# Hybrid attention and convolution encoder on one core: the first norm in fewer steps, identity products moved, the fifth weights' rounding amid the logarithms, and VectorE's order around unit 3

## The reference

```python
def encoder_layer(x, ...):
    h = rmsnorm(x, norm_mix)
    proj = einsum('btd,de->bte', h, w_in)
    q, k, v, r, g_lr, hy_in = split(proj, ...)
    o_gla = gla_group(q, k, v, r, g_lr, ...)     # gates: log_sigmoid(z @ w + b) / 16, cumulative sums
    o_hy = hyena_group(hy_in, ...)               # filters: hid = sin(freq * (feats @ w1 + b1)), twice
    x = x + einsum('bte,ed->btd', concatenate([o_gla, o_hy]), w_out)
    h = rmsnorm(x, norm_ffn)
    return x + (silu(h @ w_gate) * (h @ w_up)) @ w_down
```

## Time and profile before

| | us |
|---|---|
| median of 3 runs | 1246.21 (1244.27 to 1246.93) |
| the profiled execution, its own time | 1245.52 |
| its span (first to last instruction) | 1243.7 |
| TensorE busy | 1227.4 |
| GpSimd, ScalarE, VectorE busy | 756.9, 729.1, 726.2 |

### The profile page before, as it was taken

One profiled execution on the slowest core, in us unless ns is written; L12 is line 12 of the kernel. 1 busy time (PEld: TensorE's weight loads), 2 busy tenths in 40 slices (PEclk: granted clock), 3 DMA queues, 4 the chain that ended last, 5 costly groups with the idle time before them and its releaser, 6 DMA issues.

```text
span 1243.7 us, 21588 instructions
## 1 busy us (share of the span) xinstructions
PE 1227.4 (99%) x8224; PEld 1022.6 (82%) x8224; DVE 726.2 (58%) x1072; ACT 729.1 (59%) x1345; POOL 756.9 (61%) x618
## 2 busy tenths in 40 slices
PE   8999999999999999999999999999999999999997
PEld 6767787889988888888887777788898888888886
DVE  6846576677777777300068465664867777760004
ACT  6766655448577767532266756554576777763333
POOL 3755653547488667866527666328265666778661
PEclk9999999999999999999999999999999999999999
DMA  6211111251323322332222212114122222324232
GB/s 240 81 52 53 69 52 69 69 191 52 102 103 103 102 102 85 118 104 97 97 77 69 69 52 70 67 54 141 63 86 102 103 102 103 116 77 139 92 102 85
DMA packets 31496, 115.31 MB, mean 93 GB/s; under 512 B 3489, under 2 KB 4001, under 8 KB 31010
## 3 DMA queue, kind: packets, MB, share of 16 engines
q1 hardware_dynamic: 31394, 113.93, 26.6%
HBM read 111.82 MB, written 2.10 MB: 92 GB/s over the span
## 4 chain that ended last, share of the span: by engine, by line
PE 86%; DVE 8%; ACT 4%; issue 2%; POOL 0%; DMA 0%; POOLq 0%; ACTq 0%; DVEq 0%
PE ps L2166 19%; PE ps L2173 11%; PE ps L2006 6%; PE ps L2025 6%; PE ps L2028 6%; PE ps L2026 6%; PE ps L2008 6%; PE ps L2007 6%; PE ps L2332 2%; PE ps L2318 2%; PE ps L2019 2%; PE ps L2017 2%; PE ps L2022 2%; PE ps L2192 1%; PE ps L2169 1%
## 5 line engine op out<-in xcount | busy, mean ns | idle before, releaser
L1257 POOL TENSOR_TENSOR w_lo<-w_raw,w_hi 128x1024 fp32r<-128x1024 f32 x104 | 254.7, 2450 | 260.3 <-ACT w_hi L716 203.5
L716 ACT ACTIVATE w_hi<-w_raw 128x1024 fp32r<-128x1024 f32 x108 | 114.0, 1056 | 173.8 <-PE ps L2028 157.8
L2166 PE MATMUL ps<-h_parts,w_hi 128*128 128x512 f32 x576 | 204.9, 398 | 0.0
L2173 PE MATMUL ps<-h_parts,w_lo 128*128 128x256 f32 x672 | 188.8, 281 | 0.0
L2006 PE MATMUL ps<-h_parts,w_hi 128*128 128x512 f32 (+1 forms) x392 | 166.2, 424 | 1.9 <-POOL w_lo L1257 1.0
L2166 PE MATMUL ps<-sum_parts,w_hi 128*128 128x512 f32 x432 | 156.3, 402 | 0.0
L2008 PE MATMUL ps<-h_parts,w_lo 128*128 128x512 f32 (+1 forms) x392 | 151.9, 388 | 0.0
L2007 PE MATMUL ps<-h_parts,w_hi 128*128 128x512 f32 (+1 forms) x392 | 151.3, 386 | 0.0
L2173 PE MATMUL ps<-sum_parts,w_lo 128*128 128x256 f32 x528 | 148.4, 281 | 0.0
L1262 POOL TENSOR_TENSOR w_lo<-w_raw,w_hi 128x512 fp32r<-128x512 f32 x60 | 77.7, 1296 | 97.6 <-ACT w_hi L702 97.6
L702 ACT ACTIVATE w_hi<-ps 128x512 fp32r<-128x512 f32 x160 | 94.6, 597 | 61.0 <-DVE ps L1518 39.0
(11 more groups left out here) (300 smaller groups left out, 2844.1 us busy)
## 6 DMA issues: line engine op xcount, KB each, us to landing
w_raw<-in_units SPq DMA_DIRECT2D x110, 512.0 KB, 3.2
u<-in_pairs SPq DMA_DIRECT2D x44, 512.0 KB, 3.9
w_raw<-in_pairs SPq DMA_DIRECT2D x40, 512.0 KB, 4.1
x<-in_x SPq DMA_DIRECT2D x4, 512.0 KB, 6.4
gain<-in_gain SPq DMA_DIRECT2D x4, 512.0 KB
spec<-in_pairs SPq DMA_DIRECT2D x4, 512.0 KB, 5.1
out_y<-x SPq DMA_DIRECT2D x3, 512.0 KB, 2.6
par<-in_par SPq DMA_DIRECT2D x1, 1214.5 KB, 8.0
```

The costliest lines, as they stand in the source:

```text
L716: nc.scalar.activation(w_tile(g, 0), w_raw[:, g % RAW], ACT.Copy).then_inc(s_hi, 1)
L1257: nc.gpsimd.tensor_tensor(w_tile(g, 1), w_raw[:, g % RAW], w_tile(g, 0).bitcast(F32), ALU.subtract).then_inc(s_lo, 1)
L2166: nc.tensor.matmul(both(m, p).rearrange("p (v t) -> p v t", v=2), hi[:, cols], factor[m][:, :, k], start=start and k == 0, stop=False, ski ...
L2173: last = nc.tensor.matmul(both(m, p)[:, FIRST] if p >= WIDE else out, lo[:, cols], factor[m][:, 0, k], start=False, stop=k == KT // 2 - 1, ...
```

## The change

Six things are different.

- The first norm: `first_square` squares a whole tile of 1024 columns in one instruction, `first_root` takes the root of sum/1024 + eps with eps from a column that GpSimd sets; VectorE's mean step is gone.
- ScalarE's order at the start: w_hi of unit 0 ahead of the roundings of tiles 0 and 1, w_hi of unit 1 behind the rounding of tile 3.
- TensorE: identity products 2, 4, 4 in place of 8, 2, 8 around the first transposes; the turns of tiles 2 and 3 both behind the first half of unit 0, then five identity products into bank 1, the second half, and only then the first product of the filter network.
- The 1 MB of constants (`K_DFT` on) is issued behind the load of unit 2's weights and so behind that load's wait.
- w_hi of unit 4 is made between the Exp and the Ln of `gate_logs` in layer 0.
- VectorE, slot 2: first the unit with index 2 (the third; q) is emptied, then comes the first scan pair, then the second range reduction (layer 0), then the second scan pair.

```diff
+                if L == 0 and n == RAW:
+                    sp.dma_start(cst[:, K_DFT:N_CST], cst_d[:, K_DFT:N_CST]).then_inc(s_dft, 16)
...
+            def first_square(tt):
+                act.wait_ge(s_x[tt], 16)
+                nc.scalar.activation(g12[:, D_MODEL * tt:D_MODEL * tt + D_MODEL], x[:, tt], ACT.Square,
+                                     accum_out=ss[:, 2 * tt:2 * tt + 1]).then_inc(xsq.sem, 2)
+
+            def first_root(tt):
+                act.wait_ge(xsq.sem, xsq.at(0, 2 * tt + 2))
+                nc.scalar.activation(rs[:, tt:tt + 1], ss[:, 2 * tt:2 * tt + 1], ACT.Sqrt,
+                                     bias=rs[:, TT:TT + 1], scale=1.0 / D_MODEL).then_inc(xrt.sem, 1)
...
                 for tt in range(2):
-                    x_square(0, tt)
-                    x_root(0, tt)
+                    first_square(tt)
+                    first_root(tt)
+                hi_unit(0)
                 x_round(0, 0)
-                hi_unit(0)
                 x_round(0, 1)
                 for tt in range(2, TT):
-                    x_square(0, tt)
-                    x_root(0, tt)
+                    first_square(tt)
+                    first_root(tt)
                 x_round(0, 2)
+                x_round(0, 3)
                 hi_unit(1)
-                x_round(0, 3)
...
+                if L == 0:
+                    hi_unit(LOGS_UNIT)
                 for h in range(HEADS):
                     act.wait_ge(acs.sem, a - (HEADS - 1 - h))
...
-                    if L == 0 and slot == 2:
-                        reduce_turn(L, 1, P, net_bank(L, 1), C_B2, C_F2)
...
+                    if KINDS[slot][0] in ("q", "k"):
+                        evacuate(L, slot)
                     if slot == 2:
                         gate_sums(L, 0)
-                    if KINDS[slot][0] in ("q", "k"):
-                        evacuate(L, slot)
+                        if L == 0:
+                            reduce_turn(L, 1, P, net_bank(L, 1), C_B2, C_F2)
...
-            keep_warm(8)
+            keep_warm(2)
             x_turn(0, 0)
-            keep_warm(2)
+            keep_warm(4)
             x_turn(0, 1)
-            keep_warm(8)
+            keep_warm(4)
...
-                        first_unit(2 * L, g, 0, 0, None if L else 2)
+                        first_unit(2 * L, g, 0, 0)
+                        if L == 0:
+                            x_turn(0, 2)
                         x_turn(2 * L, TT - 1)
                         if L == 0:
-
-                            pe.wait_ge(xlo.sem, xlo.at(0, 5))
-                            net_one(0)
+                            keep_warm(5, 1)
```

More of the change, by code:

```diff
@@ L50 @@
 GROUP = 3
+LOGS_UNIT = 4
 OUT_BANKS = ((2, 3), (4, 5), (0, 1), (6, 7))
@@ L602, in _ @@
             sp.dma_start(par[:, C_MISC:N_PAR], par_d[0][:, C_MISC:N_PAR]).then_inc(s_filt, 16)
-            sp.dma_start(cst[:, K_DFT:N_CST], cst_d[:, K_DFT:N_CST]).then_inc(s_dft, 16)
             def wait_item(L, j):
@@ L716, in hi_unit @@
                 nc.scalar.activation(w_tile(g, 0), w_raw[:, g % RAW], ACT.Copy).then_inc(s_hi, 1)
+            def first_square(tt):
[6 more added lines that the diff above has]
+                                     bias=rs[:, TT:TT + 1], scale=1.0 / D_MODEL).then_inc(xrt.sem, 1)
             def x_square(b, tt):
                 for n in range(2):
[L721 to L726, removed]
+                    act.wait_ge(xres.sem, xres.at(b - 1, 2 * tt + n + 1))
+                    junk = ps[:, norm_banks(b)[tt][n], :]
                     nc.scalar.activation(junk, x[:, tt, half(n)], ACT.Square,
@@ L730, in x_root @@
             def x_root(b, tt):
-                act.wait_ge(xpre.sem, xpre.at(b, tt + 1))
+                act.wait_ge(xpre.sem, xpre.at(b - 1, tt + 1))
                 act.wait_ge(xsq.sem, xsq.at(b, 2 * tt + 2))
@@ L1100, in _ @@
                     factors(L, slot, False)
-                    hi_unit(L * UNITS + slot + 2)
+                    if L * UNITS + slot + 2 != LOGS_UNIT:
+                        hi_unit(L * UNITS + slot + 2)
                     factors(L, slot, True)
@@ L1363, in exponents @@
                     nc.gpsimd.tensor_tensor(d[:, :, 1], b[:, :, 1], m, ALU.subtract).then_inc(expo.sem, 1)
+            nc.gpsimd.memset(rs[:, TT:TT + 1], EPS)
             nc.gpsimd.memset(ones[:, :], 1.0).then_inc(s_ones, 1)
@@ L1657, in norm_start @@
                 for tt in range(2):
-                    x_mean(0, tt)
                     x_scale(0, tt)
@@ L2029, in rows, with first_unit @@
                 return last
-            def first_unit(b, g, bank, n, amid=None):
+            def first_unit(b, g, bank, n):
                 pe.wait_ge(s_lo, g + 1)
@@ L2035, in first_unit @@
                 for k in range(KT):
-                    if k == KT // 2 and amid is not None:
-                        x_turn(b, amid)
                     if k % 4 == 0:
@@ L2053, in x_turn, with keep_warm @@
                         t.then_inc(s_unit, 1)
-            def keep_warm(n):
+            def keep_warm(n, bank=6):
                 for _ in range(n):
-                    nc.tensor.matmul(ps[:, 6, 0:P], ident, ident, start=True, stop=True)
+                    nc.tensor.matmul(ps[:, bank, 0:P], ident, ident, start=True, stop=True)
             def net_one(L):
@@ L2410, in _ @@
                         first_unit(2 * L, g, 0, 1).then_inc(s_unit, 1)
+                        if L == 0:
+                            net_one(0)
                         side(L, t, 0)
```

## The result

The changed kernel takes 1251.47 us, the median of 5 runs (1250.54 to 1252.95), against 1246.21 (1244.27 to 1246.93, 5 runs) before. The ratio is 1.0046, with a 95% interval of 1.0034 to 1.0059: slower by about half a percent. The forecast had the sign, but its 1248.7 is 2.8 too low and its range ended at 1251.0. The profiled execution took 1250.54 us, the fastest of the five, with a span of 1248.8, so the span grew by 5.1 us.

A forecast was written before the change was run, and what follows sets the result against it. TensorE was taken as the bound, its level products waiting on VectorE, ScalarE and GpSimd: 39.8 + 7.5 + 4.1 = 51.4 against 48.89, so +2.5 us on 1245.52 gives 1248.0, median 1248.7; range 1245.0 to 1251.0.

The forecast's parts named there:

- The start: First norm and unit 0: first half at 12.9 instead of 15.26, second at 19.0, lead of 1.6 us at unit 1.
- The turns: VectorE and GpSimd alternate on SBUF after layer 0's first scan pair: delays 0.6 + 2.05 + 0.8, level products at 51.4.
- T: End of layer 0's first scan pair on VectorE, forecast at 39.8 against 40.40 before.
- Rival A: Layer 0's clip slips through ahead of unit 5's w_lo: 0 to −1.0 us, 1245.2 to 1246.2; chance 0.20.
- Rival C: Whole lead survives because the level products are bound by TensorE alone: −2.6 us, 1243.6; chance 0.06.
- Rival D: First range reduction also blocked, by unit 3's w_lo: T 40.2, total +2.9 to +3.0; forecast with it 0.46.
- the Sum: Total +2.5 us on the profiled 1245.52 gives 1248.0; runs' median 0.7 above, so 1248.7.
- rival B: TensorE's clock falls behind the 4.8 us idle before the level products: 1.8 us added, 1250.5; 0.28 for both cases.
- last sign of being wrong: On TensorE: forecast wrong if passes behind the idle stretch take twice as long.
- The other case of B: First unit starts at the lower clock with ten identity products instead of eighteen: same price, 1.8 us; 0.28 for both.
- Layer 1 at nothing: Layer 1's reorder costs nothing: 1.2 us of slack before L2217 cover 0.4 to 0.9 from one held scan.
- The logarithms' copy at nothing: Moving unit 4's w_hi before the four Ln pays nothing alone; needed so its w_lo is not last after the earlier emptying.

The follow-up runs named there:

- e7: Changed kernel with VectorE's old order and the old place of unit 4's w_hi copy, so only the start is new: 1243.93 us, ratio 0.9989 to the kernel before.
- e3: Changed kernel plus a GpSimd wait holding unit 5's w_lo until layer 0's second scan pair is done: 1247.78 us, ratio 1.0019 to the kernel before.
- e4: Changed kernel plus 36 identity passes on TensorE between unit 4 and layer 0's level products: 1249.24 us, ratio 1.0036 to the kernel before.
- e10: Kernel before with only the copy of unit 4's weights moved amid the logarithms: 1248.84 us, a single execution.
- e5: Changed kernel with VectorE's old order put back in layer 1 alone: 1250.62 us, a single execution.
- e1: Changed kernel with VectorE's old slot 2 order back in both layers, start and logarithms' copy still changed: 1248.83 us, ratio 1.0036 to the kernel before.

## Why the prediction was wrong in its size

**The start held.** First half 13.12 for 12.9, second 19.15 for 19.0, unit 2 at 30.34 for 30. At unit 1 the lead was 1.4 instead of 1.6. The kernel e7 shows that this part alone is a gain, 1.6 us at the end. The prediction had no price for it by itself, since it took the level products to be bound by VectorE's chain; it did not ask what the start does to that chain, which in e7 comes 1.6 us earlier because the first clip is free.

**The turns held, to a few tenths.** The forecast had the second pair's end at T+7.5; with T = 38.95 + 1.28 = 40.23 it ended at 47.84, T+7.6. The fused steps took 1.94 (0.6 more than their own), the clip 2.37, the pair 2.07 for its 1.27, as worked out. The level products followed 4.1 behind the pair (51.90). e3 took the cause away and got the time back. Rival A, in which the clip slips through, is out: the w_lo began 0.36 us before it. T itself was 0.4 late. That is a term of the sum that was mis-sized, the emptying's start at 36.13 for 35.7, and the level products' +2.5 became +3.0. Rival C is out too. Rival D did not happen: the first clip, at 26.50, took 0.29 us, 0.12 ahead of the w_lo of 26.62, so the T that D also named (40.2) has the other cause. The blocked steps agree with the Trainium skill, "SBUF — State Buffer", section "Who interferes with whom", whose page adds that issue order decides who blocks: in e7 it is the w_lo of 26.75 that comes second, and the clip ahead of it is not held.

**The step that failed is the Sum.** It took +2.5 us as the total and put the price of the clock behind the idle stretch at nothing in it, keeping it as a separate case, rival B, with 0.28. But the forecast itself contained the 4.8 us of idle TensorE on which B hangs (it was 4.9), so B was no alternative to it but its consequence, open only in whether the clock falls. It fell in the changed kernel, and the fill of e4 took that away: 1.5 us (1.8 in the prediction). Passes that take twice as long behind the idle stretch were the prediction's own last sign of being wrong. The sum of forecast and B, 1250.5, was there as B's time; with 0.4 more for T, 0.6 more for layer 1 and 0.3 less for the clock it makes 1251.2, against the 1251.47 measured. The other case of B, a first unit at the lower level, did not come: its passes of 256 columns start 0.12 us apart behind ten identity products as they did behind eighteen. The Trainium skill, "TensorE: Matmul & The Clock Gate", section "What's actually happening", has 1.2 GHz return after idleness. The traces agree: 0.51 granted behind 4.9 us of idle TensorE.

**Layer 1 at nothing was wrong.** The 1.2 us of slack ahead of L2217 were real, and the delay did not grow there (4.5 just before and at it). It grew at L2259, behind them: the first pair comes later in the new order, GpSimd's sums and w_lo with it, one w_lo meets a later pair, and the query that L2259 needs is late (1.5 us of wait for 0.8). The prediction covered one scan and did not follow the queues further.

**The logarithms' copy at nothing was wrong** for the copy alone: +3.3 in e10. In the full change it is a help, as the text said it was needed, though not for its reason (the emptying) alone: it clears the first scan pair (+9.8 without it, +5.1 with it).

The account of the 5.1 us, by the profiled executions: +3.0 to the level products, of which e3 takes away 2.9; +1.5 for the clock behind them; +0.6 in layer 1. The start's lead is no term of it, since even without the collision the chain reaches the level products no earlier than before (+0.1 in e3).

**Open.** The fall of the clock differs from one execution to another: e3, whose profiled execution shows no low stretch around its 2.0 us idle, ran from 1245.61 to 1249.59, at mean clocks of 0.996 to 0.999, so its median lies 1.7 above the profiled one. That the clock falls in those executions is argued from the mean clocks, not shown. The same holds for the changed kernel: its profiled execution has the highest mean clock of the five (0.998, the others 0.995 to 0.997), so in the median execution the clock's part is probably more than 1.5 us, and the 1251.2 above may owe some of its closeness to luck. Nor was the full change tried with w_lo(5) held, TensorE filled and layer 1 back together; from e3 and e5 it would be near the kernel before and not near e7, since e3's chain reaches the level products no earlier than before.

## What to carry to other kernels

When an edit moves work by a microsecond or two, list for VectorE and GpSimd every pair of operations that read SBUF and now fall together, over all the stages behind it, not only at the edit: here a w_lo that was issued first held a 0.3 us step for up to 2.5 us, and the versions that differ in which steps it caught, and in the idle time and low clock that followed, lie between 0.9989 and 1.0068 of the time. If your forecast contains an idle stretch of TensorE, what the clock does behind it is part of the forecast's sum, not a rival. And test parts alone before keeping a bundle: the start gains 1.6 us, and both of its companions lose by themselves (+7.2 and +3.3).

## What was unexpected in the hardware

A cast of 128x160 elements to 8 bits is also caught: in e7's VectorE timeline above it is issued at 20.30 and takes 2.17 us, while GpSimd makes w_lo(1), which began at 19.96; in the kernel before, at 22.17 with GpSimd idle, it took 0.23. The emptying instructions, which read PSUM, are never held: in all fourteen profiles each takes 0.7 us.

After about the same idle stretch (4.93 and 4.92 us) the clock was back at 2.4 GHz by 56 us in the changed kernel, while in e5 it was already at half at 50 us, during the wait, and still at 54 to 56. The loss behind the wait was 1.5 us in one and 2.0 in the other (from +3.0 to +4.5, and from +3.1 to +5.2). And a shorter stretch is enough: in e1 the clock fell (0.71 granted from 44 to 46, 0.50 from 46 to 48) behind 3.25 us idle ahead of unit 4.
